# Merged delta-rule and attention stage: triangular joins in small blocks, side products over two banks, another order of the stage's work

## The reference, cut to what matters

```python
m = jnp.einsum('nbhik,nbhjk->nbhij', kb, kc) * decay            # kb = kc * beta
a = jnp.where(idx[:, None] > idx[None, :], m, 0.0) + jnp.eye(C)
rhs = jnp.concatenate([vc * bc[..., None], kb * jnp.exp(gcum)[..., None]], axis=-1)
sol = lax.linalg.triangular_solve(a, rhs, left_side=True, lower=True, unit_diagonal=True)
u, w = sol[..., :DV], sol[..., DV:]
def step(S, inp):                                                # chunk after chunk
    v_new = u_i - jnp.einsum('bhck,bhkv->bhcv', w_i, S)
    o_i = (q_i * jnp.exp(g_i)) @ S + (q_i @ k_i.T * d_i) @ v_new
    S = S * jnp.exp(g_last) + (k_i * jnp.exp(g_last - g_i)).T @ v_new
# attention, per head and block of 128 queries, causal
p = jax.nn.softmax(s, axis=-1)                                   # two maps
amap = p[:, :, 0] - lam * p[:, :, 1]
```

## Time and profile before

| | |
|---|---|
| median of 3 runs | 1739.87 us (1738.96 to 1742.27) |
| profiled execution | 1737.59 us, span 1736.0 us |
| merged stage in the span | about 422 to 708.5 us |
| busy in the whole span | TensorE 93%, VectorE 57%, ScalarE 30%, GpSimd 18% |
| the chunks' part of the stage, first join to last multiply | 463.27 to 700.92 us |

### The profile page before, as it was taken

How to read it: one execution, slowest core, us unless ns; L and a number is a source line. 1 busy time by engine, 2 the same in 40 slices (tenths; PEclk the granted TensorE clock), 3 DMA queues, 4 the chain that set the end, 5 groups by cost and what they waited for, 6 DMA issues and landing times.

```text
span 1736.0 us, 27804 instructions
## 1 busy us (share of the span) xinstructions
PE 1620.5 (93%) x10602; PEld 1537.1 (89%) x10602; DVE 993.0 (57%) x1417; ACT 525.1 (30%) x810; POOL 313.5 (18%) x717
## 2 busy tenths in 40 slices
PE   5999999898799999687699999999999999999998
PEld 5899999897688888463599999999999999999997
DVE  4554379787566556345434655466565554665654
ACT  4343333333344343431322312121122121211214
POOL 2200056554422522432000000000000000000000
PEclk9999999999899999878799999999999999999999
DMA  4321121232123110553422121011010210110104
GB/s 145 125 55 43 37 52 38 75 99 86 32 51 107 37 44 17 178 190 97 157 57 62 39 71 49 24 60 60 24 60 13 71 48 24 60 60 24 49 0 110
DMA packets 151572, 114.29 MB, mean 66 GB/s; under 512 B 26027, under 2 KB 139197, under 8 KB 150070
## 3 DMA queue, kind: packets, MB, share of 16 engines
q1 hardware_dynamic: 145842, 101.35, 19.7%
q0 software_dynamic: 2304, 8.39, 1.4%
q10 hardware_dynamic: 3350, 3.53, 0.6%
HBM read 90.59 MB, written 21.74 MB: 65 GB/s over the span
## 4 chain that ended last, share of the span: by engine, by line
PE 49%; DVE 1%; ACT 1%; issue 0%; DMA 0%; SPq 0%; ACTq 0%; DVEq 0%
PE f_up L2961 28%; PE f_down L2968 14%; PE f_up L185 4%; PE f_up L2921 1%; PE f_up L2948 1%; PE f_up L2968 0%; PE f_up L3006 0%; DVE h_rstd L2801 0%; DMA f_rows<-in_ffn_conv_b 0%; DVE o_lo L2781 0%; PE f_up L2995 0%; PE f_down L2911 0%; ACT f_tail_tok L2729 0%; DVE w_lo L2750 0%; DVE dn_lo L2892 0%
## 5 line engine op out<-in xcount | busy, mean ns | idle before, releaser
L2961 PE MATMUL f_up<-h_hi,w_hi 128*128 128x352 f32 x1032 | 335.1, 325 | 1.9 <-DVE w_lo L2750 1.2
L2961 PE MATMUL f_up<-h_hi,w_lo 128*128 128x352 f32 x1032 | 333.4, 323 | 0.0
L2961 PE MATMUL f_up<-h_lo,w_hi 128*128 128x352 f32 x1032 | 333.4, 323 | 0.0
L185 PE MATMUL proj<-x_hi,win_hi 128*128 128x352 f32 x672 | 219.3, 326 | 5.3 <-issue 3.0
L185 PE MATMUL proj<-x_hi,win_lo 128*128 128x352 f32 x672 | 216.6, 322 | 0.0
L185 PE MATMUL proj<-x_lo,win_hi 128*128 128x352 f32 x672 | 216.2, 322 | 0.0
L2961 PEld LDWEIGHTS f_up<-h_hi,w_hi 128*128 128x128 f32 x1032 | 193.8, 188 | 2.5 <-DVE w_lo L2750 1.5
L2961 PEld LDWEIGHTS f_up<-h_hi,w_lo 128*128 128x128 f32 x1032 | 194.1, 188 | 0.0
L2961 PEld LDWEIGHTS f_up<-h_lo,w_hi 128*128 128x128 f32 x1032 | 193.8, 188 | 0.0
L2968 PE MATMUL f_down<-f_g_hi,dn_hi 128*128 128x352 f32 x512 | 165.3, 323 | 0.0
L2968 PE MATMUL f_down<-f_g_hi,dn_lo 128*128 128x352 f32 x512 | 164.7, 322 | 0.0
(11 more groups left out here) (439 smaller groups left out, 2948.7 us busy)
## 6 DMA issues: line engine op xcount, KB each, us to landing
w_raw<-in_w_up SPq DMA_DIRECT2D x44, 512.0 KB, 3.9
win_raw<-in_w_in SPq DMA_DIRECT2D x28, 512.0 KB, 4.1
dn_raw<-in_w_down SPq DMA_DIRECT2D x11, 1024.0 KB, 5.1
p_key<-in_cache_k SPq DMA_DIRECT2D x32, 256.0 KB, 3.7
feat<-in_cache_v POOLq DMA_DIRECT2D x24, 256.0 KB, 5.1
x_scratch<-feat SPq DMA_DIRECT2D x1, 4224.0 KB, 13.4
feat<-x_scratch SPq DMA_DIRECT2D x8, 528.0 KB, 8.8
feat<-in_x_prompt SPq DMA_DIRECT2D x8, 512.0 KB, 8.3
```

The costliest lines, as they stand in the source:

```text
L185: mm = nc.tensor.matmul(out, w[:, k, :], x[:, k, g * TG:(g + 1) * TG], start=(k == 0 and i == 0), stop=(k == KT - 1 and i == 2))
L2961: mm = nc.tensor.matmul(up[u % RING][:, 0:TG], a[s][:, kk, :], b, start=(kk + x == 0), stop=(kk == KT - 1 and x == 2))
```

## The change

- `AT_off` is one tile, for level 0 alone, cut by four transfers per chunk (the upper 16 rows of each 32 x 32 diagonal block) where seven were. Levels 1 and 2 read AT itself.
- `join` and `extend` multiply only the blocks that matter: 32 x 32 blocks at levels 0 and 1, 64 x 64 at level 2, each written to the partitions of its own rows. `keep_M` copies and `extended` subtracts the matching pieces.
- `spread_decay`, `spread_beta` and `keys_queries` go to `chain[0]` and no longer to `side`; joins and `solve_u` wait for those who read them there.
- TensorE's order in a step is now: join or solve_u, cumulate, state_w, state_out, turn_keys, keys_keys, **extend** or solve_w, spread_beta, **scores**, turn_map 0, state_next, keys_queries, spread_decay, turn_values, turn_map 1, multiply. At the end `state_out` comes ahead of `state_next`.
- `keys_by_token` and `values_by_token` move from VectorE (three instructions of [128, 512] per chunk) to ScalarE (twelve of [128, 128], with a per-partition scale). VectorE calls `extended` ahead of `maxima`.

```diff
+                for q in QUADS:
+                    sp.dma_start(AT_off[first_half(q), :, second_half(q)], AT[n % 2][first_half(q), :, second_half(q)]).then_inc(cut, 16)
@@ spread_beta
+                    pe.wait_ge(u_kept, n - 1)
@@ turn_values
-                    pe.wait_ge(AT_ready, n + 2)
+                    pe.wait_ge(KE_ready, n + 2)
@@ join
                 if level == 0:
+                    pe.wait_ge(cut, 16 * len(QUADS) * (n + 1))
                     pe.wait_ge(DD_in, 16 * (n + 1))
+                    if n + 1 < NC:
+                        pe.wait_ge(AT_ready, n + 2)
+                if level == 2 and n + 1 < NC:
+                    pe.wait_ge(PT_ready, n + 2)
                 for h in range(H):
-                    mm = nc.tensor.matmul(chain[0][:, h * P:(h + 1) * P], AT_off[level][:, h, :], D(n)[:, h, :], start=True, stop=True)
+                    for rows in blocks_of(level):
+                        one, two = first_half(rows), second_half(rows)
+                        if level == 0:
+                            mm = nc.tensor.matmul(chain[0][rows, cols(h, 16)], AT_off[rows, h, rows], D(n)[rows, h, one],
+                                                  start=True, stop=True)
+                        else:
+                            mm = nc.tensor.matmul(chain[0][two, cols(h, 16 << level)], AT[n % 2][one, h, two], D(n)[one, h, one],
+                                                  start=True, stop=True)
@@ extend
+                b = 16 << level
+                for h in range(H):
+                    for rows in lower_blocks(level):
+                        at = rows if level == 0 else second_half(rows)
+                        nc.tensor.matmul(chain[1][at, cols(h, b)], DT(n)[at, h, at], M[at, cols(h, b)], start=True, stop=True)
+                    for rows in blocks_of(level):
+                        at = rows if level == 0 else second_half(rows)
+                        mm = nc.tensor.matmul(chain[1][first_half(rows), cols(h, b, H * HALF)], M[at, cols(h, b)],
+                                              DT(n)[at, h, second_half(rows)], start=True, stop=True)
@@ solve_u
+                if n + 2 < NC:
+                    pe.wait_ge(arg_ready, n + 3)
+                    pe.wait_ge(e_row_ready, n + 3)
@@ ScalarE
+            def keys_by_token(n):
+                act.wait_ge(kt_done, n + 1)
+                act.wait_ge(beg_ready, n + 1)
+                act.wait_ge(ET_ready, n + 1)
+                for h in range(H):
+                    ins = nc.scalar.activation(kbg[n % 2][:, h, :], side[:, h * P:(h + 1) * P], ACT.Copy, scale=beg[:, h:h + 1])
+                ins.then_inc(kbg_ready, 1)
+                for h in range(H):
+                    ins = nc.scalar.activation(kdec[n % 2][:, h, :], side[:, h * P:(h + 1) * P], ACT.Copy, scale=ET[:, h, P - 1:P])
+                ins.then_inc(kdec_ready, 1)
@@ ScalarE's order in a step
+                t = chunk_at(n, p, "turn_keys", 2, 1)
+                if t is not None:
+                    keys_by_token(t)
                 if last is not None:
                     keep_map(last, 0)
...
                     keep_map(last, 1)
-                if a is not None:
-                    exps(a, 1)
                 t = chunk_at(n, p, "spread_decay", 2, 2)
                 if t is not None:
                     decays(t)
+                t = chunk_at(n, p, "turn_values", 3, 1)
+                if t is not None:
+                    values_by_token(t)
+                if a is not None:
+                    exps(a, 1)
```

More of the change, by code:

```diff
@@ L1055, in delta_and_attention @@
     beg_ready, qg_ready = sem("c_beg_ready"), sem("c_qg_ready")
-    cut = [sem(f"c_cut{level}") for level in range(NLV)]
+    cut = sem("c_cut")
     C_done, R_done, KK_done, B_done, KQ_done, kt_done, vt_done = (
@@ L1162, in _ @@
                 if n == 0:
[L1163 to L1168, removed]
+                    sp.wait_ge(off_zero, 1)
+                else:
+                    sp.wait_ge(M_done, NLV * (n - 1) + 1)
+                for q in QUADS:
+                    sp.dma_start(AT_off[first_half(q), :, second_half(q)], AT[n % 2][first_half(q), :, second_half(q)]).then_inc(cut, 16)
                 if n == 0:
@@ L1422, in _ @@
             for n, p, a, last in plan:
+                if n < 0 and a is not None:
+                    scores(a)
                 if n >= 0:
@@ L1432, in _ @@
                     cumulate(t)
+                if n >= 1 and p == 0:
+                    state_w(n - 1)
+                if n >= 1 and p == 1:
+                    state_out(n - 1, side)
                 t = chunk_at(n, p, "turn_keys", 2, 1)
@@ L1438, in _ @@
                     keys_keys(t)
-                if n >= 1 and p == 0:
-                    state_w(n - 1)
-                if n >= 1 and p == 1:
-                    state_out(n - 1)
-                if n >= 0 and a is not None:
-                    scores(a)
                 if n >= 0:
@@ L1449, in _ @@
                         solve_w(n)
-                if last is not None:
-                    turn_map(last, 0)
                 t = chunk_at(n, p, "spread_beta", 3, 2)
@@ L1454, in _ @@
                     spread_beta(t)
+                if n >= 0 and a is not None:
+                    scores(a)
+                if last is not None:
+                    turn_map(last, 0)
+                if n >= 1 and p == 0:
+                    state_next(n - 1)
                 t = chunk_at(n, p, "keys_queries", 1, 1)
@@ L1460, in _ @@
                     spread_decay(t)
-                if n >= 1 and p == 0:
-                    state_next(n - 1)
-                if last is not None and groups_of(last) == 2:
-                    turn_map(last, 1)
                 t = chunk_at(n, p, "turn_values", 3, 1)
@@ L1467, in _ @@
                     turn_values(t)
+                if last is not None and groups_of(last) == 2:
+                    turn_map(last, 1)
                 if last is not None:
@@ L1470, in _ @@
             state_w(NC - 1)
+            state_out(NC - 1, chain[0])
             state_next(NC - 1)
-            state_out(NC - 1)
         @block.scalar
@@ L1512, in keep_M @@
                 act.wait_ge(M_done, NLV * n + level + 1)
-                nc.scalar.copy(M[:, :, :], heads(chain[0][:, :])).then_inc(M_kept, 1)
+                if level == 0:
+                    ins = nc.scalar.copy(M[:, 0:H * 16], chain[0][:, 0:H * 16])
+                else:
+                    for rows in blocks_of(level):
+                        kept = slice(0, H * (16 << level))
+                        ins = nc.scalar.copy(M[second_half(rows), kept], chain[0][second_half(rows), kept])
+                ins.then_inc(M_kept, 1)
             def keep_u(n):
@@ L1574, in keys_decayed @@
                 if n >= 2:
[L1575 to L1576 removed]
+                    dve.wait_ge(cut, 16 * len(QUADS) * (n - 1))
+                    dve.wait_ge(M_done, NLV * (n - 1))
                     dve.wait_ge(at_out, 16 * (n - 1))
@@ L1654, in _ @@
             for n, p, a, last in plan:
-                if n < 0 and a is not None:
+                if n < 0 and p != 0 and a is not None:
                     maxima(a)
@@ L1665, in _ @@
                     keys_decayed(t)
-                if n >= 0 and a is not None:
-                    maxima(a)
-                if n >= 0 and p < NLV:
-                    extended(n, p)
                 t = chunk_at(n, p, "spread_beta", 3, 2)
@@ L1672, in _ @@
                     keys_weighted(t)
+                if (n >= 0 or p == 0) and a is not None:
+                    maxima(a)
                 t = chunk_at(n, p, "keys_queries", 1, 1)
```

141 lines of the change are left out of this document (74 added, 67 removed).

## The result

The changed kernel takes **1746.12 us** (median of 15 runs, 1741.95 to 1752.39) where the kernel before takes 1739.89 (15 runs, 1735.39 to 1743.78): ratio **1.0035**, 95% interval [1.0023, 1.0048]. It is slower by 6 us; 9 us less were forecast.

The account below looks back on a forecast made before the run. TensorE's work was taken to bound the chunks, with waits between. Terms of -30 (work), -9 (waits going), +27 (new waits), +1 (early steps) and +2 (tail) summed to -9 us, forecasting 1731 us, range 1710 to 1752.

Parts of the forecast that it names:

- TensorE's work: Joins and extensions in the chunks: small blocks side by side save 3.7 us per chunk, -30 us in all.
- Waits that go and come: TensorE's waits, mostly in the chunks: -9 us for those that go, +27 us for new ones.
- (a): Step p = 1: the level 2 join waits for queries_decayed (PT), behind maxima in VectorE; +6.6 us.
- (b): Step p = 0, chunks 4 to 7: state_out waits for the next state behind the same maxima; +4.7 us.
- (c): From p = 3 into p = 0, chunks 0 to 2: state_w waits for vb, level 0 extension for M; +6.4 us.
- (d): Large unit's difference ends late, new_values behind it, so state_next waits in chunks 1 and 2; +2.7 us.
- (e): Extensions have too little work between them and their joins to cover keep_M; +3.8 us.
- (f): Scalings ahead of keep_map at p = 2, solve_u's earlier decay wait in chunk 4, chunk 6's uncovered last map; +3 us.
- waits give way: Rival: the new waits do not add, 12 of 27 us remain, giving -24 us, 1716; chance 0.22.
- ScalarE and VectorE set the pace: Rival: in steps with large units all that TensorE saves is waited out, nothing changes, 1740 us; chance 0.16.
- One after another: Rival: small products in all six groups of a chunk run in series, +8 us, 1748; chance 0.22.
- as costly as whole ones: Rival: each small product of joins and extensions costs what a whole one does, +50 us, about 1790; chance 0.03.

Follow-up runs that it names:

- whole_in_new_order: The changed kernel with joins and extensions of whole 128 x 128 matrices as before; order, banks and ScalarE scalings stay: 1752.36 us, ratio 1.0068.
- blocks_alone: The kernel before with only the block joins and extensions added, old order, banks and VectorE scaling kept: 1741.05 us, ratio 0.9998.
- tokens_and_filler: The changed kernel with the token scalings back on VectorE and ten groups of four unused whole products at TensorE's waits: 1729.3 us, ratio 0.9933.
- filler: The changed kernel with 13 groups of four unused whole products where TensorE stood waiting: 1741.28 us, ratio 1.0002.
- blocks_and_filler: The kernel before with block joins and extensions, plus ten groups of four unused whole products: 1733.87 us, ratio 0.997.
- filler_small: The changed kernel with unused 32 x 32 block products, 48 or 24 at each of 13 TensorE waits: 1753.29 us, ratio 1.0076.
- tokens_on_vector: The changed kernel with keys_by_token and values_by_token back on VectorE; blocks, banks and order stay: 1738.34 us, ratio 0.9993.

## Why the prediction was wrong, point by point

**The step that failed** is in the sum: every term is priced at the upper level, because the chunks of before stood at 0.98 to 1.00, as if the clock were a property of the stage and not of the work in it. For the chunks, the lower clock appears in the prediction only under "what would show it", as a clock under 0.95, with no price, no rival and no chance; only the early steps had an uncertainty for it. It came out as 0.92, and it costs +16.5 us by the account of the windows and 12 by the slope of the runs; with either the sum -9 becomes +3 to +8, and +6 was measured. That the blocks bring it is shown: whole_in_new_order has after's order and is never low in the chunks, blocks_alone has before's order and is low for 41 us, and the mean clocks of all their runs say the same (0.974 and 0.962). That it costs time is shown by tokens_and_filler, where added whole products shorten the program beyond the intervals; filler and blocks_and_filler go the same way with intervals that overlap at their edges, and in filler_small, with small products added, the program is not shorter. What exactly the chip weighs is not shown: the blocks also make TensorE less busy, and only filler_small speaks for the kind of product.

**TensorE's work, -30 us**: right, -31.1 at equal clock. The parts were off in both directions by little. In chunk 2 joins and extensions, taken to the start of what follows, need about 0.34 + 0.57 + 0.37 + 0.38 + 0.57 + 0.61 = 2.84 us, changes of block size among them, where 2.5 + 0.9 were counted; eight chunks at that rate would save 34 us, and 31 were saved. From the last small row of level 1's join (548.80) to the next whole product it is 0.12 us, the 0.1 of the prediction.

**Waits that go and come, +18**: right as a sum (+19.1) and in most terms. (a) PT: 5.2 us idle, from start to start 6.0; 6.6 forecast. (b) next state: 5.2 and 5.5; 4.7 forecast. (c) `state_w` and M: 4.9 + 1.6; 6.4 forecast. (d) `state_next` waits 1.2 us for vn, and `turn_map` waits for the same `difference` 3.2 us more than before: 4.4 together, 2.7 forecast. (e) extensions wait for M in the later levels: 1.3; 3.8 forecast. (f) `solve_u` in chunk 4, 1.5, and the copies of the map, 3.2 more than before: 4.7; 3 forecast. So the sum is right in part because errors of single terms cancel.

**VectorE and ScalarE**: ScalarE is busy 49% of the chunks (51 forecast). Four copies for vb take 1.15 us to their end, and `keep_M` is small, as the groups of after show:

```profile
L1591 ACT ACTIVATE c_vb<-c_side,ba 128x128 f32<-128x128 f32 x28 | 8.1, 386 | 0.0
...
L1561 ACT COPY c_M<-c_chain 32x128 f32<-32x128 f32 x16 | 4.1, 258 | 1.0 <-PE c_chain L1351 0.6
L1561 ACT COPY c_M<-c_chain 64x256 f32<-64x256 f32 x8 | 2.9, 368 | 2.3 <-PE c_chain L1351 2.3
```

**Ends**: early -0.4 (+1 forecast), tail +1.6 (+2).

**The rivals.** That waits give way fell (+19 stayed). That ScalarE and VectorE set the pace fell as it was put: fillers at the waits would then have added nothing at best. One part holds: the scalings on ScalarE cost 8 us against VectorE, most of it by way of the clock if the slope is taken. One after another, and as costly as whole ones, fell with the timeline. The result lies on the side of the slower rival, but not by its mechanism.

**The clock's penalty.** After is low for 37.6 us more than before. The Trainium skill ("TensorE: Matmul & The Clock Gate", Terms) puts the penalty at about the low time times the share of the clock that is missing. By it, the estimate is 37.6 x 0.5 = 18.8 us. The account's 16.5 agrees, since TensorE was idle for a tenth of the low time; the slope of the runs gives less, 12.

**What stays open.** Why the low stretches begin where they do: they move from kernel to kernel. And the split of tokens_on_vector's gain between shorter waits and clock is only by the slope.

## What to carry to other kernels

When a change takes TensorE work away in a phase at the upper clock, or cuts it into small blocks, put a term for the lower level into the sum, and read the granted clock of the stretch before any group. Here it took back half of a saving of 31 us. Two tests are cheap: unused whole products at the waits (a shorter time together with a higher clock points to the clock), and the new order with the old products (which separates waits from clock).

## What the runs showed of the hardware

- Sixteen f32 products of 32 x 32 blocks with 16 columns, in four diagonal places of the array and into one bank, start within 0.27 us.
- Groups of small products, about 1 us at each of 13 waits, left the mean clock at 0.960 (0.961 without them); whole ones at the same places raised it to 0.966.
- The kernel with the most TensorE work in the chunks (219.5 us busy) has the highest mean clock of all, 0.974, and the new waits (idle 30.3 us, more than before's 20.8) did not lower it.
- Runs of one and the same kernel differ by 0.008 in mean clock, and by 10 us with it (correlation -0.91 over 35 runs): most of the scatter of this kernel's times goes with the clock.
